# Query blocks and gate-half blocks in products of 512 columns, evacuated by two engines

## The reference

```
def gmlp_chunk_mix(h, w_uv, v_norm, w_s, b_s, w_o):
    z = jax.nn.gelu(h @ w_uv)
    u, v = jnp.split(z, 2, axis=-1)
    v = rms_norm(v, v_norm)
    ...
    sv = jnp.einsum('gts,bcsgd->bctgd', ws, v) + jnp.transpose(b_s)[:, :, None]
    ...
    return (u * sv) @ w_o

def memory_cross_attention_2(h, mem_k, mem_v, wq, wo):
    q = (h @ wq).reshape(B, S, XATTN_HEADS, XATTN_HEAD_DIM)
    s = jnp.einsum('bshd,bmhd->bhsm', q, mem_k).astype(jnp.float32) * (XATTN_HEAD_DIM ** -0.5)
    p = jax.nn.softmax(s, axis=-1).astype(h.dtype)
    o = jnp.einsum('bhsm,bmhd->bshd', p, mem_v).reshape(B, S, C)
    return o @ wo
```

## Time and profile before

| | |
|---|---|
| median of 3 timed runs | 1893.21 us (1893.11 to 1893.58) |
| profiled execution | 1896.16 us |
| its span in the trace | 1894.4 us |
| granted TensorE clock, mean | 0.997 |
| stretch of attention x0 (queries to the last head's output) | about 1060 to 1100 us |
| stretch of the gated mixing | about 1493 to 1637 us |
| stretch of attention x1 | about 1637 to 1677 us |

### The profile page before, as it was taken

One profiled execution on the slowest core, in us unless ns is written; L12 is line 12 of the kernel. 1 busy time (PEld: TensorE's weight loads), 2 busy tenths in 40 slices (PEclk: granted clock), 3 DMA queues, 4 the chain that ended last, 5 costly groups with the idle time before them and its releaser, 6 DMA issues.

```text
span 1894.4 us, 37276 instructions
## 1 busy us (share of the span) xinstructions
PE 1852.8 (98%) x15522; PEld 1699.0 (90%) x15522; DVE 1380.2 (73%) x1829; ACT 1088.6 (57%) x1474; POOL 45.1 (2%) x42
## 2 busy tenths in 40 slices
PE   7999998999999999999999999999999999999998
PEld 7998998899999888998887998888888889998887
DVE  6687589779888777699755668766776657658764
ACT  6566576766666554468533555545554574556553
POOL 0000000000000000000151000000000000000000
PEclk9999999999999999999999999999999999999999
DMA  6854333355554555544300535554555554535553
GB/s 227 243 176 159 134 135 112 135 199 178 192 185 157 199 192 188 185 154 150 135 25 20 187 125 184 195 186 175 191 193 194 178 184 172 178 112 190 188 198 113
DMA packets 52334, 313.64 MB, mean 166 GB/s; under 512 B 13536, under 2 KB 13792, under 8 KB 14944
## 3 DMA queue, kind: packets, MB, share of 16 engines
q1 hardware_dynamic: 51760, 308.42, 46.2%
q10 hardware_dynamic: 432, 3.15, 0.4%
HBM read 310.50 MB, written 1.05 MB: 164 GB/s over the span
## 4 chain that ended last, share of the span: by engine, by line
PE 84%; DVE 11%; ACT 3%; issue 2%; DMA 1%; DVEq 0%; SPq 0%; ACTq 0%
PE ps L311 32%; PE ps L398 20%; PE ps L401 10%; PE ps L536 9%; PE ps L533 4%; DVE wl L2476 4%; PE ps L926 1%; ACT wh L1618 1%; PE ps L941 1%; DVE pages L3137 1%; PE ps L1198 1%; DMA raw<-in_stream 1%; PE ps L889 0%; DVE pages L3002 0%; DVE pages_r L2499 0%
## 5 line engine op out<-in xcount | busy, mean ns | idle before, releaser
L2476 DVE TENSOR_TENSOR wl<-raw,wh 128x1024 fp32r<-128x1024 f32 x576 | 698.1, 1225 | 316.0 <-ACT wh L1618 309.8
L1618 ACT ACTIVATE wh<-raw 128x1024 fp32r<-128x1024 f32 x575 | 600.6, 1055 | 430.4 <-DMA raw<-in_stream 165.2
L398 PE MATMUL ps<-norm_r,wh 128*128 128x512 f32 x1760 | 443.1, 393 | 1.2 <-DVE wl L2476 0.7
L398 PEld LDWEIGHTS ps<-norm_r,wh 128*128 128x128 f32 x1760 | 316.4, 189 | 58.6 <-DVE wl L2476 1.1
L311 PE MATMUL ps<-pages_r,wh 128*128 128x256 f32 x1776 | 342.9, 285 | 14.9 <-DVE wl L2476 14.1
L311 PE MATMUL ps<-norm_r,wh 128*128 128x256 f32 x1632 | 302.7, 285 | 0.2
L311 PEld LDWEIGHTS ps<-pages_r,wh 128*128 128x128 f32 x1776 | 284.3, 192 | 17.9 <-DVE wl L2476 12.1
L311 PE MATMUL ps<-pages_r,wl 128*128 128x256 f32 x976 | 276.8, 284 | 0.0
L311 PEld LDWEIGHTS ps<-norm_r,wh 128*128 128x128 f32 x1632 | 256.0, 192 | 3.1 <-issue 1.9
L401 PEld LDWEIGHTS ps<-norm_r,wl 128*128 128x128 f32 x1760 | 240.8, 190 | 17.6
L401 PE MATMUL ps<-norm_r,wl 128*128 128x256 f32 x1760 | 246.2, 282 | 0.0
(11 more groups left out here) (354 smaller groups left out, 1955.0 us busy)
## 6 DMA issues: line engine op xcount, KB each, us to landing
raw<-in_stream SPq DMA_DIRECT2D x287, 1024.0 KB, 4.8
pages<-in_rpb SPq DMA_DIRECT2D x32, 64.0 KB, 6.0
pages<-in_mem SPq DMA_DIRECT2D x2, 512.0 KB, 6.7
raw<-in_stream SPq DMA_DIRECT2D x2, 512.0 KB, 8.9
x<-in_x SPq DMA_DIRECT2D x1, 1024.0 KB, 12.7
pages<-in_mem ACTq DMA_DIRECT2D x1, 1024.0 KB, 4.9
pages<-in_gmlp_b ACTq DMA_DIRECT2D x1, 1024.0 KB, 4.6
pages<-in_gmlp_w ACTq DMA_DIRECT2D x1, 1024.0 KB, 7.9
```

Of the source, the lines that this page charges most:

```text
L398: mm = pe.matmul(ps[:, bank + j, :], wh[:, cols], t.norm_r[:, 2 * k * T:2 * (k + 1) * T], start=k == 0, stop=False, skip_group_check=True)
L1618: f(t.wh[(2 * b0 + hf) % PIECE_SLOTS][:], t.raw[b0 % 2][:, hf * 1024:(hf + 1) * 1024], ACT.Copy).then_inc(s["high_done"], 1)
L2476: tt(t.wl[i][:], t.raw[b0 % 2][:, hf * 1024:(hf + 1) * 1024], t.wh[i][:].bitcast(F32), ALU.subtract).then_inc(s["low_done"], 1)
```

## The change

The four query blocks of both memory attentions, the two blocks of gm_u and the six of gm_w are made with `wide_block` (by the new `wide_project`), so each takes two banks, and `SEGMENTS` counts two banks for each. To take a block out, ScalarE copies the half that lies in columns T to 2T of the two banks to SBUF (`proj_crossed`, signal `proj_cross`), VectorE adds the half in columns 0 to T (`proj_whole`, which frees both banks) and then multiplies by `t.rstd` in SBUF (`spread`, `gate_scale`), which signals `proj_in`; `scores` and `gate_gelu` wait for `proj_in`. Adds come ahead of the wait for the norm factor for blocks 0 and 1 of each group, multiplications behind it. In the loop of the gated mixing VectorE's order stays, ScalarE's becomes: high(gm_w 1+k) half 0, gate_gelu(2+k) for k < 4, high half 1, half_crossed(3+k), gate_gelu(3+k) for k >= 3, then gated_high(q) as before.

```
+    def wide_project(seg, first=0, n=4, name=None):
+        for k in range(first, first + n):
+            at_ = SEG[seg] + 2 * k
+            wide_block(at_, at_ % BANKS, BLK[seg] + k, None if k else name)
...
     def memory_attention(i, name):
-        project(f"xq{i}", norm_parts, n=1, name=name)
-        project(f"xq{i}", norm_parts, first=1, n=1)
+        wide_project(f"xq{i}", n=2, name=name)
         norm_sum(name)
-        project(f"xq{i}", norm_parts, first=2, n=1)
+        wide_project(f"xq{i}", 2, 1)
...
+    def proj_crossed(seg, k, dst):
+        bank = (SEG[seg] + 2 * k) % BANKS
+        act.wait_ge(s["piece_done"], 2 * (BLK[seg] + k) + 2)
+        f(tiles(dst, 2), ps[:, bank:bank + 2, T:2 * T], ACT.Copy).then_inc(s["proj_cross"], 1)
...
         exp(0)
         highs(f"xq{i}", 3, 1)
+        query_crossed(i, 3)
         exp(1)
...
         late_norm(f"x{i}", prev)
-        highs(f"xq{i}", n=2)
+        highs(f"xq{i}", n=1)
+        query_crossed(i, 0)
+        highs(f"xq{i}", 1, 1)
+        query_crossed(i, 1)
         norm_root(f"x{i}")
         highs(f"xq{i}", 2, 1)
+        query_crossed(i, 2)
...
     high(BLK["gm_w"])
-    gate_gelu(2)
+    half_crossed(2)
     for k, behind in enumerate(MIX_BEHIND):
-        high(BLK["gm_w"] + 1 + k)
-        gate_gelu(3 + k)
+        high(BLK["gm_w"] + 1 + k, (0,))
+        if k < 4:
+            gate_gelu(2 + k)
+        high(BLK["gm_w"] + 1 + k, (1,))
+        half_crossed(3 + k)
+        if k >= 3:
+            gate_gelu(3 + k)
         for q in behind:
             gated_high(q)
...
+    def proj_whole(seg, k, dst):
+        bank = (SEG[seg] + 2 * k) % BANKS
+        dve.wait_ge(s["proj_cross"], proj_at(seg, k) + 1)
+        link(tt(tiles(dst, 2), ps[:, bank:bank + 2, 0:T], tiles(dst, 2), ALU.add))
+        dve.sem_inc(s["u_evac"], 2)
...
+    def gate_scale(k):
+        made = t.pages[:, k * 512:(k + 1) * 512]
+        scaled(made, tiles(made, 2), 2).then_inc(s["proj_in"], 1)
+
+    def gate_half(k):
+        gate_whole(k)
+        gate_scale(k)
```

More of the change, by code:

```diff
@@ L93 @@
     ("w_out", 4, 4), ("ffn0", 44, 33), ("ffn1", 44, 33), ("mem2_k", 4, 4), ("rw_k", 4, 4), ("mem2_u", 1, 1), ("lora", 0, 1),
-    ("rw_r", 4, 5), ("lora2", 0, 1), ("mem2_v", 3, 3), ("rw_v", 4, 4), ("rw_o", 4, 4), ("xq0", 4, 4), ("xo0", 4, 4),
-    ("ffn2", 44, 33), ("ffn3", 44, 33), ("gm_u", 2, 2), ("gm_v", 8, 8), ("gm_w", 6, 6), ("gm_o", 4, 8),
-    ("xq1", 4, 4), ("xo1", 4, 4), ("ffn4", 44, 33),
+    ("rw_r", 4, 5), ("lora2", 0, 1), ("mem2_v", 3, 3), ("rw_v", 4, 4), ("rw_o", 4, 4), ("xq0", 8, 4), ("xo0", 4, 4),
+    ("ffn2", 44, 33), ("ffn3", 44, 33), ("gm_u", 4, 2), ("gm_v", 8, 8), ("gm_w", 12, 6), ("gm_o", 4, 8),
+    ("xq1", 8, 4), ("xo1", 4, 4), ("ffn4", 44, 33),
 ]
@@ L122 @@
 att_low zero_row inner_zero hidden_made hidden_high crossed att_high att_gates norm_sq norm_part acc_done norm_sum
-norm_var norm_std norm_out x_up gate_ready gate_scaled hidden_ready conv_cross conv_u conv_mid gelu_ready dve_chain
+norm_var norm_std norm_out x_up gate_ready gate_scaled hidden_ready conv_cross conv_u conv_mid gelu_ready proj_cross proj_in dve_chain
 att_scores att_max att_exp att_prob att_turned att_turned_sb att_out lb_zero lb_exp bias_ready conv_done
@@ L126 @@
 hg_o hg_sq hg_var hg_varsb hg_std hg_out merged lora_mid lora_out rw_mix rw_kk2 rw_kksum rw_kkfloor
-rw_kkln rw_kkvar rw_kkn rw_bonus_in rw_bonus_sum rw_bonus_sb rw_cum rw_exp rw_dec rw_t rw_t_sb rw_lx rw_mb rw_rk rw_lt rw_lx_read rw_xx
+rw_kkln rw_kkvar rw_kkn rw_bonus_in rw_bonus_sum rw_bonus_sb rw_cum rw_exp rw_dec rw_t rw_t_sb rw_lx rw_lt rw_lx_read rw_xx
 rw_plain rw_masked rw_lm rw_phase rw_pass rw_xt rw_y rw_y_sb rw_z rw_z_sb rw_zt_sb rw_rhs0 rw_rhs1 rw_rhs_sb0 rw_rhs_sb1 rw_u0 rw_u1 rw_u_sb0 rw_u_sb1 rw_centre
@@ L1172, in scores @@
         def scores(h):
-            pe.wait_ge(s["u_evac"], SEG[f"xq{i}"] + h + 1)
+            pe.wait_ge(s["proj_in"], proj_at(f"xq{i}", h) + 1)
             for qb in range(TB):
@@ L1204, in memory_attention @@
     def memory_attention(i, name):
-        project(f"xq{i}", norm_parts, n=1, name=name)
-        project(f"xq{i}", norm_parts, first=1, n=1)
+        wide_project(f"xq{i}", n=2, name=name)
         norm_sum(name)
-        project(f"xq{i}", norm_parts, first=2, n=1)
+        wide_project(f"xq{i}", 2, 1)
         scores, turn, mix = memory_heads(i)
         scores(0)
-        project(f"xq{i}", norm_parts, first=3, n=1)
+        wide_project(f"xq{i}", 3, 1)
         scores(1)
@@ L1238, in tensor_program @@
     swiglu(3, "ffn3", "ffn3")
-    project("gm_u", norm_parts, n=2, name="mix2")
+    wide_project("gm_u", n=2, name="mix2")
     pe.wait_ge(s["norm_part"], 2 * NORM["mix2"] + 2)
@@ L1267, in mix_pair @@
         mm.then_inc(s["gm_mix"], 1)
-    project("gm_w", norm_parts, n=2)
+    wide_project("gm_w", n=2)
     pe.wait_ge(s["gm_mask"], 1)
@@ L1272, in tensor_program @@
     for k in range(2, 6):
-        project("gm_w", norm_parts, first=k, n=1)
+        wide_project("gm_w", k, 1)
         mix_quarters(MIX_BEHIND[k - 1])
@@ L1377, in conv_in, with proj_at @@
     return t.page[13][:, k * 1024 + half * 512:k * 1024 + (half + 1) * 512]
+def proj_at(seg, k):
+    order = [("xq0", 4), ("gm_u", 2), ("gm_w", 6), ("xq1", 4)]
+    at_ = 0
+    for name, n in order:
+        if name == seg:
+            return at_ + k
+        at_ += n
 def first_spare(t, hf):
@@ L2365, in memory_heads, with query_crossed @@
         out(3)
+    def query_crossed(i, k):
+        proj_crossed(f"xq{i}", k, t.page[0][:, k * 512:(k + 1) * 512])
     def memory_attention(i, prev=None):
         late_norm(f"x{i}", prev)
-        highs(f"xq{i}", n=2)
+        highs(f"xq{i}", n=1)
+        query_crossed(i, 0)
+        highs(f"xq{i}", 1, 1)
+        query_crossed(i, 1)
         norm_root(f"x{i}")
         highs(f"xq{i}", 2, 1)
+        query_crossed(i, 2)
         memory_heads(i)
@@ L2380, in scalar_program, with half_crossed @@
     late_norm("mix2", last_down(3), (3,))
-    highs("gm_u", n=2)
+    def half_crossed(k):
+        seg, n = ("gm_u", k) if k < 2 else ("gm_w", k - 2)
+        proj_crossed(seg, n, t.pages[:, k * 512:(k + 1) * 512])
+    for k in range(2):
+        highs("gm_u", k, 1)
+        half_crossed(k)
     act.preload_act_table_set("natural_log_exp_and_others")
@@ L2390, in gate_gelu @@
         c = slice(k * 512, (k + 1) * 512)
-        act.wait_ge(s["u_evac"], (SEG["gm_u"] + k if k < 2 else SEG["gm_w"] + k - 2) + 1)
+        act.wait_ge(s["proj_in"], proj_at("gm_u", k) + 1)
         f(t.pages[:, c], t.pages[:, c], ACT.Gelu_apprx_tanh).then_inc(s["gm_up"], 1)
@@ L3367, in memory_attention, with whole, spread, query @@
         late_norm(f"x{i}", prev)
-        lows(f"xq{i}", n=2)
-        dve.wait_ge(s["norm_std"], NORM[f"x{i}"] + 1)
[L3371 to L3380, removed]
+        def whole(k):
+            low(BLK[f"xq{i}"] + k)
+            proj_whole(f"xq{i}", k, t.page[0][:, k * 512:(k + 1) * 512])
+        def spread(k):
+            made = t.page[0][:, k * 512:(k + 1) * 512]
+            scaled(made, tiles(made, 2), 2).then_inc(s["proj_in"], 1)
+        def query(k):
+            whole(k)
+            spread(k)
+        whole(0)
+        whole(1)
+        dve.wait_ge(s["norm_std"], NORM[f"x{i}"] + 1)
+        spread(0)
+        spread(1)
+        query(2)
         memory_heads(i, query)
@@ L3387, in vector_program, with gate_whole @@
     late_norm("mix2", last_down(3))
-    lows("gm_u", n=2)
-    dve.wait_ge(s["norm_std"], NORM["mix2"] + 1)
[L3391 to L3399, removed]
+    def gate_whole(k):
+        seg, n = ("gm_u", k) if k < 2 else ("gm_w", k - 2)
+        proj_whole(seg, n, t.pages[:, k * 512:(k + 1) * 512])
+    def gate_scale(k):
+        made = t.pages[:, k * 512:(k + 1) * 512]
+        scaled(made, tiles(made, 2), 2).then_inc(s["proj_in"], 1)
+    def gate_half(k):
+        gate_whole(k)
+        gate_scale(k)
+    for k in range(2):
+        lows("gm_u", k, 1)
+        gate_whole(k)
+    dve.wait_ge(s["norm_std"], NORM["mix2"] + 1)
+    gate_scale(0)
+    gate_scale(1)
     dve.wait_ge(s["rows_in"], 32)
```

## The result

The changed kernel takes 1906.52 us (median of 4 runs, 1905.18 to 1908.02) against 1893.39 us (1893.11 to 1894.42) before: ratio 1.0071, 95% interval 1.0059 to 1.0083, so 13.1 us slower. The profiled execution took 1908.02 us, its span is 1906.2 us.

A forecast was written before the change was run, and what follows sets the result against it. TensorE (98% busy) bounds the kernel before, ScalarE and VectorE in turn the changed mixing loop. +10.4 us there and +0.1 in the attentions make +10.5, from the median 1893.21 to 1903.7; range 1901.5 to 1907.5.

The forecast's parts named there:

- The turn of the loop: Gated-mixing loop: ScalarE and VectorE each wait for the other once, a turn of 8.83 us, 10.94 with two quarters.
- The waits: TensorE's waits for VectorE's low parts between gm_w3 and gm_o1: 0.75, 1.45, 4.46 and 4.66 us.
- The small fifth wait: In gm_o, behind its second block: TensorE waits 0.35 us for the mixed product's last operand quarters.
- The clock: Behind the mixing's two long waits: whether a fall of TensorE's clock adds 1.7 us; the forecast of 1903.7 adds none.
- rival 1: Behind the mixing's long waits the clock falls and is paid for: +1.7 us, 1905.4 or up to 1907; chance 0.26.
- net +0.04 us an attention: Chain behind query block 3: the add costs 0.69 us, four wide blocks give 0.65 back.
- The attentions: Both memory attentions: +0.1 us together, TensorE's wait for the first turned probabilities going from 1.1 to 1.8 us.
- gm_u: Two wide blocks, where VectorE and ScalarE have idle time: −0.33 us.
- The savings: Wide blocks take 5.59 us in place of 5.75, 0.16 less each; 16 blocks save 2.6 us of TensorE.
- the 2.93 us: ScalarE's stand before each gated_high in the kernel before, read as time in which a weight copy behind could run.
- Rival 2: Mixing loop stays under TensorE's 6.5 to 7.4 us a turn: 1892.0, or 1890.6 with the adds hidden; chance 0.1.

The follow-up runs named there:

- e2: Changed kernel with the attentions' query blocks back to narrow, so the change in the mixing alone: 1906.9 against 1894.07 us before, ratio 1.0066.
- e1: Changed kernel with gm_u and gm_w back to narrow, so the change in the attentions alone: 1895.39 against 1894.07 us before, ratio 1.0004.
- e3: Changed kernel with products of zeros in TensorE's new waits, to keep it active: 1904.74 against 1894.07 us before, ratio 1.0056.
- e7: e2 with ScalarE's and VectorE's work in the gm_w loop in another order: 1893.08 against 1893.31 us before, ratio 0.9998.
- e5: Kernel before, narrow products, but ScalarE copies gate-half banks out in the changed order and VectorE only multiplies: 1902.81 against 1893.46 us, ratio 1.0048.
- e6: Kernel before with one spare VectorE addition behind each of eight gate-half multiplications: 1894.43 against 1893.46 us, ratio 1.0.
- e4: Changed kernel, same work, with e7's order in the mixing and a new order in the attentions: 1890.8 against 1894.07 us before, ratio 0.9983.
- e8: e1 with e4's order in the attentions, mixing as before: 1890.72 against 1893.46 us before, ratio 0.9984.
- e9: e8 with the two gm_u blocks wide in addition, gm_w narrow: 1891.62 against 1893.46 us before, ratio 0.9989.

## Why the prediction held, and where its size was off

**The turn of the loop: right.** 8.91 and 11.03 us against 8.83 and 10.94 worked out. The difference of 0.08 is in the main one step: from the add to the multiplication behind it 0.84 us (1571.73 to 1572.57), where I had put 0.72; the other steps were together 0.04 shorter.

**The waits: right in place and order.** 0.66, 1.30, 4.25 us against 0.75, 1.45, 4.46. The fourth was 2.43 in place of 4.66, for the reason that stood among the rivals: behind the third wait the clock fell, the first half of the output quarter took 8.03 us (1594.43 to 1602.46) in place of 5.75, and 4.66 − 2.28 = 2.4 was left. Whatever the clock cost there the wait paid back. e2 shows the same exchange with other numbers: its clock was low for half as long behind the third wait (1.7 us lost), and its fourth wait was 2.99 us. The small fifth wait (0.35 us, for the last operand quarters) didn't come.

**The clock: the forecast chose wrongly.** It put 0.6 on a clock that costs nothing on the path (1903.7) and 0.26 on the rival at 1905.4 to 1907; the median is 1906.5. So the loop was foreseen, but that the time lies inside the range is owed to the rival's end of it: the forecast with its 1.3 us ends at 1905.0. Behind the fourth wait TensorE ran low: from 1604.89 to ScalarE's release at 1612.4 it took 7.5 us for 5.75, 1.75 us, as rival 1 priced a drop. What neither case had was a drop in the attentions. There the step "net +0.04 us an attention" looked at the chain alone; with the wait grown from 1.1 to 1.9 us the clock fell behind both in the profiled execution. The first was 60.4 before, 62.6 with the drop and 60.9 without (e1, e3). It doesn't come each time (x1 of e1), which may be why filling the waits (e3) brought 1.8 to 2.5 us in the timed runs and not the 4.4 of the stages; that isn't shown, since one run of each kernel was profiled.

**The attentions: right but for 0.15 us.** +0.2 each without a drop, from +0.5 in the stage less 0.33 for the first two blocks; the wait was 1.9 for 1.8. The same step of 0.84 in place of 0.69 is the difference.

**gm_u: right.** From behind ffn2's sum to behind mix2's 372.9 us for 373.2 to 374.1.

**The savings: right.** 5.59 us a block, at 1.84 and 0.95 us for eight products.

**Two readings that were loose.** ScalarE's weight copies in the kernel before were not free of VectorE: they stood behind gated_high even then. What was new is that VectorE waits for ScalarE too. And the 2.93 us for which ScalarE stood before gated_high don't show a copy held up behind it. In the chain of waits the products of that copy's block lie here, and ScalarE went on like this (kernel before):

```profile
1576.69 5.75 PE ps L311 x48
```
```profile
1581.56 0.63 ACT L2420 ACTIVATE pages_r<-pages 128x512 fp32r<-128x512 f32 x1 [1.48 <-DVE pages L3429]
1582.10 1.99 ACT L1618 ACTIVATE wh<-raw 128x1024 fp32r<-128x1024 f32 x2
```

The copy's slot came free with the first half of the block, at 1579.56 (1576.69 and half of 5.75), after the 2.93 us. The 1.48 us of the second gated_high are the ones in which a copy was held up.

**Rival 2 (the loop keeps up): wrong for this order, right for another.** It was refused because of the order in which gated_high stands. With gated_high a turn later and the crossing and the low parts moved with it (e7) the loop does keep up. What I had said decides, the length of a turn, does decide.

## What to carry to other kernels

When a step that one engine did alone is split over two, look at what stands ahead of the first half in its queue and whether any of that waits for the second engine; if it does, a turn of the loop becomes the sum of both engines' work, and the shares of the whole span don't show it (58% and 73% here, with 8.9 us turns for 6.5 us of products). In e7 the cure cost no work: the item that waits (gated_high) came one turn later, behind the new step, and the new step ahead of work that can follow it. Then count the busiest engine again in that stage alone, since it may have no room left for the gain.

## What the runs showed of the hardware that was not expected

A single wait of 1.9 us of TensorE, with dense products on both sides, was followed by some 3.4 us at the 1.2 GHz level in three attentions (both of the changed kernel, x0 of e1) and by none in x1 of e1. Each such drop cost the attention 1.7 us. In the attentions and the mixing of the eleven traces shorter waits were followed by none: 1.30 and 0.66 us in the mixing of the changed kernel, 1.25 in that of e5, 1.1 us in the attentions (before, e2, e5, e6, e7), 0.3 us (e4, e8, e9). All longer ones with nothing in them had a drop in or behind them: 2.3 us (e6), 2.43 and 4.25 us (changed), 2.99 and 4.25 us (e2), 3.08 us (e5). In e3, where a wait of 2.30 us was followed by 64 products of zeros, there was none.

The length of a wait doesn't settle what the drop costs either. The same 4.25 us were followed by two different drops: in the changed kernel the clock fell in the wait and was low for some 6.8 us in all (3.4 us lost, a part of it in the wait itself), in e2 it fell only as the products started again and was low for some 3.4 us (1.7 us lost). What decides between falling and staying at 1.9 us, and between the two at 4.25, the runs leave open.
